# The first expert's slots are gathered by themselves, and parts of three weight matrices are loaded by transfers of their own

## The chip, the cores and the metric

The kernel runs on one core of one Trainium2 chip. The metric is the device time of one execution in microseconds (us). TensorE has two clock levels, 1.2 and 2.4 GHz; the profile shows the level that was granted as 0.50 or 1.00.

## What is computed

Two transformer layers over 256 tokens of width 1024, all in float32. The change lies in the second layer, and almost all of it in the mixture of 32 experts at its end:

```python
def hier_moe(h, w_group, b_group, w_expert, b_expert, w1, w3, w2):
    ...
    g_sel = jnp.argmax(g_logit, axis=-1)             # one of 4 groups
    ...
    top_p, top_i = lax.top_k(jax.nn.softmax(e_logit, axis=-1), EXPERT_TOPK)   # 2 of its 8 experts
    gate = g_w * top_p / jnp.sum(top_p, axis=-1, keepdims=True)
    ...
    def expert_block(args):
        xb, e = args
        hid = jax.nn.silu(xb @ w1[e]) * (xb @ w3[e])
        return hid @ w2[e]
    ...

def hybrid_layer(x, ...):
    ...
    x = x + mixed @ w_out
    x = x + hier_moe(rms_norm(x, g_ffn), w_group, b_group, w_expert, b_expert, w1, w3, w2)
    return x
```

Each expert has an up matrix pair w1 and w3 (1024 x 512) and a down matrix w2 (512 x 1024), each 2 MB (2.10 million bytes): 192 MB for 32 experts. The second matrix of the pair, w3, is the one that the title of the change calls the up matrix.

## The kernel before

**Dense part.** Both layers up to the experts go through `unit_plan`, a list of 1 MB weight units. SyncE (the `sp` program) loads unit u into a ring of three places (`arena` slots 1 to 3) once unit u-3 has been split (`load`, which waits on `lo_ready`), ScalarE and VectorE split it into a high and a low part, and TensorE (the `pe` program) multiplies. `step_plan` puts the other steps between the units. In the second layer the units `kiwi`, `qi` x2, `kb` x2, `qb` x2, `vb` x2 and so on come first; `rope_done` counts the rotated key and query blocks that VectorE has finished (line 2004), and the fourth is that of the first `kb` unit.

**Loads of the experts.** SyncE issues all of them, in the order of its program, and each waits for its buffer. Four sets of buffers serve the first four experts: `even_w` for expert 0, `odd_w` for 1, `third_w` for 2, `fourth_w` for 3. `odd_w[1]`, for w3 of expert 1, lies in `arena` slots 0 and 1; slot 1 is one of the ring's, slot 0 is not. The down matrix of expert 3 shares its buffer (`even_w[2]`) with that of expert 0, so its load waits for `e_y` 1, the end of expert 0's last matmul. The load of the first half of expert 4's w1 waits for `e_w1_half`, the middle of expert 0's w1; the second half for `e_w1`; its w3 for `e_up` 1, the end of expert 0's w3; its w2 for `e_y` 4. From expert 8 on a loop (`stream`) issues the three matrices of one expert after another, each as soon as the expert that used the buffer is through with it.

**Experts.** They go in eight groups of four (`QUAD`), with 32 slots for tokens each. `quad_body` on TensorE first gathers the tokens of the four experts together, in 16 calls of 128 x 128 weights (`n3g`) against the 128 columns of `one_hot` (line 1302; the profile counts two records for each float32 call); ScalarE and VectorE copy the result to `xg`. Then come, for each expert, w1 and w3 (line 1358), the gates of the four experts behind the first one's w3 (`spread_gates`, line 1326) or the sum of the expert before (`add_to_tokens`, line 1342), and w2 (line 1374). The first two quads are written out, the others run in a loop. Ahead of the first quad stands the choice of the experts: 36 columns of logits (`route_logits`, line 1167), a chain on VectorE, the ranks (lines 1284 to 1288) and `one_hot` (line 2309).

## Time and profile before

| what | us |
|---|---|
| median of 3 runs | 1076.07 (1074.75 to 1076.33) |
| the profiled execution, its time | 1076.97 |
| the profiled execution, its span | 1074.9 |
| TensorE busy in the span | 932.0 (87%) |
| weights loaded into TensorE | 767.0 (71%) |
| VectorE busy | 505.0 (47%) |
| ScalarE busy | 364.1 (34%) |
| bytes moved | 310.00 MB, mean 288 GB/s |
| start of the first gather | 631.43 |
| start of the last expert's w2 | 1062.50 |

The shares are means over stages of different kinds: up to about 580 us TensorE is busy without a break and the DMA engines about half of the time; later it is the other way round. Times in the rows are from the span's start.

### The profile page before, as it was taken

Reading aid. Unit: us, or ns where it says so; the run is one execution under the profiler, and the core shown is the slowest. Engines: PE = TensorE matmul, PEld = TensorE weight load, DVE = VectorE, ACT = ScalarE, POOL = GpSimd, SP = SyncE. Lnnn points to the kernel's source line nnn. Section 1 sums busy time; section 2 is a strip of 40 time slices with the busy share of each in tenths; the row PEclk is TensorE's granted clock in tenths of the full one; section 3 lists DMA queues with packets and bytes.
Section 4 is the critical chain, followed back from the end, with each engine's and each line's share of the span. In section 5 each row is a group of like instructions: output and inputs, shape, how many; then the busy total and the mean of one; then the engine's idle time right before and its main releaser. Section 6 shows DMA issues by size and latency. Waiting matters only on the chain.

```text
span 1074.9 us, 22614 instructions
## 1 busy us (share of the span) xinstructions
PE 932.0 (87%) x9976; PEld 767.0 (71%) x9976; DVE 505.0 (47%) x812; ACT 364.1 (34%) x517; POOL 32.6 (3%) x34
## 2 busy tenths in 40 slices
PE   9999999999999999999999988886766657676754
PEld 8998877888888888989777876665545546464642
DVE  5647768687676667889877651110000100010101
ACT  6445766454444345444666330000000000000001
POOL 1200002110000001000000000000000000000000
PEclk9999999999999999999999999998888988797988
DMA  9954434545555654444457999999999999999995
GB/s 330 309 176 165 152 130 163 172 162 196 195 183 169 211 160 157 158 157 157 158 180 285 392 399 425 422 427 426 427 426 429 428 429 429 429 429 429 428 429 209
DMA packets 86830, 310.00 MB, mean 288 GB/s; under 512 B 5612, under 2 KB 46264, under 8 KB 73976
## 3 DMA queue, kind: packets, MB, share of 16 engines
q1 hardware_dynamic: 84816, 304.20, 73.4%
q0 software_dynamic: 1056, 4.20, 1.2%
q8 instruction: 42, 0.69, 0.3%
q10 hardware_dynamic: 904, 0.81, 0.2%
q14 instruction: 12, 0.10, 0.0%
HBM read 308.15 MB, written 1.05 MB: 288 GB/s over the span
## 4 chain that ended last, share of the span: by engine, by line
PE 58%; issue 38%; DVE 2%; ACT 1%; POOL 1%; ACTq 0%; POOLq 0%; DVEq 0%
PE ps L879 13%; PE ps L881 12%; PE ps L880 12%; PE ps L1003 7%; PE ps L1005 4%; PE ps L1358 1%; PE ps L1152 1%; PE ps L1374 1%; PE ps L1140 1%; PE ps L1058 1%; ACT x_both L1582 1%; PE ps L1302 0%; PE ps L1064 0%; POOL stat L816 0%; PE ps L978 0%
## 5 line engine op out<-in xcount | busy, mean ns | idle before, releaser
L1358 PE MATMUL ps<-arena,xg 128*32 128x128 f32 x2816 | 108.9, 318 | 75.1 <-DMA arena<-in_w 72.7
L1742 DVE TENSOR_TENSOR w_split<-arena,w_split 128x2048 fp32r<-128x2048 f32 x70 | 159.3, 2287 | 28.3 <-ACT w_split L1419 27.8
L2328 DVE TENSOR_TENSOR hid<-silu_e,ps 128x128 f32<-128x128 f32 x32 | 12.1, 378 | 313.6 <-ACT silu_e L1691 313.6
L1358 PEld LDWEIGHTS ps<-arena,xg 128*32 128x32 f32 x2816 | 93.4, 128 | 92.5 <-DMA arena<-in_w 86.0
L1419 ACT ACTIVATE w_split<-arena 128x2048 fp32r<-128x2048 f32 x70 | 132.7, 1900 | 66.1 <-PE ps L881 57.9
L1003 PE MATMUL ps<-x_both,w_split 128*128 128x512 f32 x352 | 124.8, 398 | 0.0
L879 PE MATMUL ps<-w_split,x_both 128*128 128x512 f32 x256 | 102.2, 399 | 0.3 <-DVE w_split L1798 0.3
L880 PE MATMUL ps<-w_split,x_both 128*128 128x512 f32 x256 | 99.8, 390 | 0.0
L881 PE MATMUL ps<-w_split,x_both 128*128 128x512 f32 x256 | 99.8, 390 | 0.0
L1005 PE MATMUL ps<-x_both,w_split 128*128 128x256 f32 x352 | 98.8, 281 | 0.0
L1374 PE MATMUL ps<-arena,hid_T 128*32 128x256 f32 x960 | 68.0, 428 | 28.1 <-DMA arena<-in_w 26.9
L1691 ACT ACTIVATE silu_e<-ps 128x128 f32<-128x128 f32 x32 | 8.9, 277 | 238.4 <-PE ps L1358 238.4
L1003 PEld LDWEIGHTS ps<-x_both,w_split 128*128 128x128 f32 x352 | 66.1, 188 | 16.4 <-issue 0.3
L1374 PEld LDWEIGHTS ps<-arena,hid_T 128*32 128x32 f32 x960 | 33.1, 120 | 57.6 <-issue 37.2
L879 PE MATMUL ps<-x_both,w_split 128*128 128x256 f32 (+1 forms) x256 | 72.9, 285 | 0.9 <-DVE w_split L1742 0.7
L881 PE MATMUL ps<-x_both,w_split 128*128 128x256 f32 (+1 forms) x256 | 72.3, 283 | 0.0
L880 PE MATMUL ps<-x_both,w_split 128*128 128x256 f32 (+1 forms) x256 | 72.3, 282 | 0.0
L879 PE MATMUL ps<-w_split,o_hi 128*128 128x512 f32 (+1 forms) x176 | 68.2, 388 | 0.5 <-DVE gates L1960 0.5
L1752 DVE TENSOR_TENSOR w_split<-arena,w_split 128x2048 fp32r<-128x2048 f32 x24 | 55.0, 2293 | 26.3 <-ACT w_split L1429 25.0
L881 PE MATMUL ps<-w_split,o_lo 128*128 128x512 f32 (+1 forms) x176 | 67.1, 381 | 0.0
L880 PE MATMUL ps<-w_split,o_hi 128*128 128x512 f32 (+1 forms) x176 | 66.9, 380 | 0.0
L1005 PEld LDWEIGHTS ps<-x_both,w_split 128*128 128x128 f32 x352 | 66.5, 189 | 0.4
(325 smaller groups left out, 1471.4 us busy)
## 6 DMA issues: line engine op xcount, KB each, us to landing
arena<-in_w SPq DMA_DIRECT2D x71, 2048.0 KB, 26.0
arena<-in_w_in SPq DMA_DIRECT2D x41, 1024.0 KB, 5.1
even_w<-in_w SPq DMA_DIRECT2D x13, 2048.0 KB, 26.4
arena<-in_w_ffn_in SPq DMA_DIRECT2D x22, 1024.0 KB, 5.1
third_w<-in_w SPq DMA_DIRECT2D x6, 2048.0 KB, 16.6
arena<-in_w_ffn_out SPq DMA_DIRECT2D x11, 1024.0 KB, 4.9
arena<-in_w_out SPq DMA_DIRECT2D x8, 1024.0 KB, 6.4
arena<-in_w SPq DMA_DIRECT2D x6, 1024.0 KB, 7.5
```

What stands on the lines that cost most here:

```text
L879: mm(dst, l_hi, r_hi, start=start, stop=False)
L880: mm(dst, l_hi, r_lo, start=False, stop=False)
L881: return mm(dst, l_lo, r_hi, start=False, stop=stop)
L1003: mm(ps[:, bank + n, :], hi[:, c, col], x_both[:, c, :, :].rearrange("p a b -> p (a b)"), start=c == 0, stop=False)
L1005: last = mm(ps[:, bank + n, 0:T], lo[:, c, col], x_hi[:, c, :], start=False, stop=c == kc - 1)
L1058: mm(ps[:, bank, 0:P], ones, ones, start=True, stop=True)
L1358: last = mm(ps[SLOTS * g:SLOTS * g + SLOTS, 6, P * n:P * n + P], xg[:, c, SLOTS * e:SLOTS * e + SLOTS], places[n][:, c, P * g:P * g + P], ...
L1374: last = mm(ps[SLOTS * g:SLOTS * g + SLOTS, 7, 0:UC], hid_T[:, SLOTS * b:SLOTS * b + SLOTS], places[2][:, b, UC * g:UC * g + UC], start=b ...
L1419: fn(w_hi[:, u % 3, 0:n], ring[:, u % 3, 0:n], ACT.Copy).then_inc(hi_ready, 1)
L1742: v.tensor_tensor(w_lo[:, u % 3, 0:n], ring[:, u % 3, 0:n], w_hi[:, u % 3, 0:n].bitcast(F32), ALU.subtract).then_inc(lo_ready, 1)
L1752: v.tensor_tensor(w_lo[:, s, :], ring[:, s, :], w_hi[:, s, :].bitcast(F32), ALU.subtract)\
L2328: v.tensor_tensor(hid[:, :].rearrange("p (b i) -> p i b", b=4), silu_e[:, :].rearrange("p (i b) -> p i b", b=4), ps[:, 6, P:2 * P].rearran ...
```

## The change

It has five parts.

1. **First gather in two.** In the first quad TensorE gathers the 32 slots of expert 0 alone (`collect(0, SLOTS)`), then does its w1, then gathers the 96 slots of experts 1 to 3 (`collect(SLOTS, P)`), then its w3. The copies to `xg` on ScalarE and VectorE are split in the same way. Later quads gather as before.
2. **First half of expert 1's w3.** Its 1 MB goes to `arena` slot 0 right behind the load of unit `kiwi` + 7 and after a wait for `rope_done` 4, early in the second layer; the second half is issued where the whole was.
3. **First quarter of expert 3's w2.** Its 0.5 MB goes to a buffer of its own, `spare_w2`, right behind the load of expert 2's w2; the other three quarters are issued where the whole was. The room comes from putting `gate_e` where `masked_e` lay.
4. **Down matrix in two transfers.** In the loop of loads, which now goes by quads (8 to 31), the w2 of each quad's last expert comes as three quarters and a last quarter; TensorE waits for the last (`last_block`) only ahead of its fourth block. These are 6 more transfers.
5. **Counts.** The waits on `xg_half`, `xg_done`, `xg_part` and `xg_ready` are one higher from the second quad on.

```diff
@@ -436,13 +436,14 @@
     logits = moe("logits", [P, TB, 36])
     exp_in = moe("exp_in", [P, TB, 36])
     exp_out = moe("exp_out", [P, TB, 36])
+    masked_at = mo
     masked_e = moe("masked_e", [P, TB, EXPERTS + 6])
     left_e = moe("left_e", [P, TB, EXPERTS + 6])
     top2 = moe("top2", [P, TB, 8])
     pick_g = moe("pick_g", [P, TB, GROUPS])
     r_s = moe("r_s", [P, 16, TB])
     chosen = moe("chosen", [P, TB, EXPERTS])
-    gate_e = moe("gate_e", [P, TB, EXPERTS])
+    gate_e = moe("gate_e", [P, TB, EXPERTS], where=masked_at)
     rank = moe("rank", [P, TB, EXPERTS])
     slot_no = moe("slot_no", [P, SLOTS])
     one_hot = moe("one_hot", [P, TB, P])
@@ -454,6 +455,8 @@
     silu_e = moe("silu_e", [P, P])
     hid = moe("hid", [P, P])
     hid_T = moe("hid_T", [P, P])
+
+    spare_w2 = moe("spare_w2", [P, D])
 
     ps = nc.alloc_psum_tensor("ps", [P, 8, 512], F32)
 
@@ -552,6 +555,8 @@
     hot_ready, xg_done, xg_ready, gt_done, gt_ready = (sem(n) for n in ("hot_ready", "xg_done", "xg_ready",
                                                                         "gt_done", "gt_ready"))
     e_w1, e_w1_half = sem("e_w1"), sem("e_w1_half")
+    last_block = sem("last_block_w2_in")
+    odd_first, spare_in = sem("odd_w3_first_half"), sem("spare_quarter_in")
     e_up, e_silu, e_hid, e_hidT, e_y, e_yA = (sem(n) for n in (
         "e_up", "e_silu", "e_hid", "e_hidT", "e_y", "e_y_act"))
     gt_rest, xg_half = sem("gt_rest"), sem("xg_half")
@@ -723,6 +728,11 @@
             landing = (first_half, landed_w[0])[half][which]
             sp.dma_start(even_w[which][:, part, :], sources[which][:, e, part, :]).then_inc(landing, 16)
 
+        def odd_half(half):
+
+            part = slice(4 * half, 4 * half + 4)
+            sp.dma_start(odd_w[1][:, part, :], sources[1][:, 1, part, :]).then_inc((odd_first, landed_w[1][1])[half], 16)
+
         for u in range(S2 + 3 * (NF - 2), U):
             if u == second_merge + 1:
                 sp.wait_ge(o_done, 20)
@@ -735,6 +745,9 @@
             elif u == out20:
                 half_load(1, 1)
             load(u)
+            if u == first["kiwi"] + 7:
+                sp.wait_ge(rope_done, 4)
+                odd_half(0)
             if u in (out20, out20 + 1):
                 if u == out20:
                     sp.wait_ge(o_done, 28)
@@ -744,7 +757,7 @@
         sp.wait_ge(sum_T, 8)
         expert_load(1, odd_w, 0, landed_w[1][0])
         sp.wait_ge(lo_ready, U - 2)
-        expert_load(1, odd_w, 1, landed_w[1][1])
+        odd_half(1)
         sp.wait_ge(unit_done, U - 2)
         expert_load(2, third_w, 0, in_third3[0])
         sp.wait_ge(lo_ready, U)
@@ -753,6 +766,7 @@
         expert_load(2, third_w, 1, in_third3[1])
         sp.wait_ge(unit_done, U)
         expert_load(2, third_w, 2, in_third3[2])
+        sp.dma_start(spare_w2[:, :], sources[2][:, 3, 0, :]).then_inc(spare_in, 16)
         sp.wait_ge(route_T, 4)
         sp.wait_ge(sq_ready, 4)
         sp.wait_ge(seeded, 4)
@@ -764,7 +778,7 @@
         sp.wait_ge(e_up, 1)
         expert_load(4, even_w, 1, landed_w[0][1])
         sp.wait_ge(e_y, 1)
-        expert_load(3, fourth_w, 2, in_fourth[2])
+        sp.dma_start(fourth_w[2][:, 1:4, :], sources[2][:, 3, 1:4, :]).then_inc(in_fourth[2], 16)
         for which in range(3):
             sp.wait_ge((e_w1, e_up, e_y)[which], 2)
             expert_load(5, odd_w, which, landed_w[1][which])
@@ -778,17 +792,22 @@
             sp.wait_ge((e_w1, e_up, e_y)[which], 6)
             expert_load(7, odd_w, which, landed_w[1][which])
 
-        def stream(pass_, lo_pair):
-
-            with sp.Fori(lo_pair, EXPERTS // 2) as i:
-                for odd in range(2):
-                    e = sp.snap(i * 2 + odd)
-                    used = sp.snap(i * 2 + (pass_ * EXPERTS + odd - 1))
+        def stream(pass_, lo_quad):
+
+            with sp.Fori(lo_quad, EXPERTS // QUAD) as i:
+                for j in range(QUAD):
+                    e = sp.snap(i * QUAD + j)
+                    used = sp.snap(i * QUAD + (pass_ * EXPERTS + j - 1))
                     for which in range(3):
                         sp.wait_ge((e_w1, e_up, e_y)[which], used)
-                        expert_load(e, (even_w, odd_w)[odd], which, landed_w[odd][which])
-
-        stream(0, 4)
+                        if (j, which) == (QUAD - 1, 2):
+                            src = sources[2][:, bass.ds(e, 1), :, :].rearrange("p e c n -> p (e c) n")
+                            sp.dma_start(odd_w[2][:, 0:3, :], src[:, 0:3, :]).then_inc(landed_w[1][2], 16)
+                            sp.dma_start(odd_w[2][:, 3:4, :], src[:, 3:4, :]).then_inc(last_block, 16)
+                        else:
+                            expert_load(e, (even_w, odd_w)[j % 2], which, landed_w[j % 2][which])
+
+        stream(0, 2)
         sp.wait_ge(passes_ready, 1)
         n_pass = sp.value_load(passes_i[0:1, 0:1], min_val=1, max_val=T // SLOTS)
         with sp.If(n_pass > 1):
@@ -1294,16 +1313,20 @@
 
             if not looped:
                 pe.wait_ge(n3_ready, 2)
-            for half in range(2):
-                for tb in range(TB):
-                    if half == 0:
-                        pe.wait_ge(hot_part, q * 2 + (tb + 1))
-                    for i in range(4):
-                        last = mm(ps[:, 4 + half, P * i:P * i + P], n3g[:, tb, 4 * half + i, :], one_hot[:, tb, :],
-                                  start=tb == 0 and i == 0, stop=tb == 1 and i == 3)
-                if half == 0:
-                    last.then_inc(xg_half, 1)
-            last.then_inc(xg_done, 1)
+            first_quad = not looped and q == 0
+
+            def collect(lo, hi):
+
+                for half in range(2):
+                    for tb in range(TB):
+                        if half == 0:
+                            pe.wait_ge(hot_part, q * 2 + (tb + 1))
+                        for i in range(4):
+                            last = mm(ps[:, 4 + half, P * i + lo:P * i + hi], n3g[:, tb, 4 * half + i, :],
+                                      one_hot[:, tb, lo:hi], start=tb == 0 and i == 0, stop=tb == 1 and i == 3)
+                    last.then_inc((xg_half, xg_done)[half], 1)
+
+            collect(0, SLOTS if first_quad else P)
 
             def place_of(e):
 
@@ -1350,10 +1373,12 @@
                 for n in range(2):
                     if not looped and e == 0 and (q == 0 or n == 0):
                         pe.wait_ge(first_half[n], 16 * (q + 1))
+                    if first_quad and (e, n) == (1, 1):
+                        pe.wait_ge(odd_first, 16)
                     pe.wait_ge(landing[n], arrived)
                     for c in range(KC):
                         if e == 0 and n == 0 and c % 4 == 0:
-                            pe.wait_ge((xg_part, xg_ready)[c // 4], q + 1)
+                            pe.wait_ge((xg_part, xg_ready)[c // 4], q + 1 if first_quad else q + 2)
                         for g in range(4):
                             last = mm(ps[SLOTS * g:SLOTS * g + SLOTS, 6, P * n:P * n + P],
                                       xg[:, c, SLOTS * e:SLOTS * e + SLOTS], places[n][:, c, P * g:P * g + P],
@@ -1361,6 +1386,11 @@
                         if not looped and q == 0 and e == 0 and n == 0 and c == KC // 2 - 1:
                             last.then_inc(e_w1_half, 1)
                     last.then_inc((e_w1, e_up)[n], 1)
+                    if first_quad and (e, n) == (0, 0):
+                        collect(SLOTS, P)
+                if e == 0 and first_quad:
+                    for half in range(2):
+                        pe.wait_ge((xg_part, xg_ready)[half], 2)
                 if e == 0:
                     spread_gates()
                 else:
@@ -1370,9 +1400,15 @@
                 pe.wait_ge(landing[2], arrived)
                 pe.wait_ge(e_hidT, done + 1)
                 for b in range(4):
+                    if looped and (e, b) == (QUAD - 1, 3):
+                        pe.wait_ge(last_block, pe.snap(q * 16 - 16))
+                    w2_block = places[2][:, b, :]
+                    if first_quad and (e, b) == (3, 0):
+                        pe.wait_ge(spare_in, 16)
+                        w2_block = spare_w2[:, :]
                     for g in range(4):
                         last = mm(ps[SLOTS * g:SLOTS * g + SLOTS, 7, 0:UC],
-                                  hid_T[:, SLOTS * b:SLOTS * b + SLOTS], places[2][:, b, UC * g:UC * g + UC],
+                                  hid_T[:, SLOTS * b:SLOTS * b + SLOTS], w2_block[:, UC * g:UC * g + UC],
                                   start=b == 0, stop=b == 3, tile_position=(0, SLOTS * g))
                 last.then_inc(e_y, 1)
             add_to_tokens(QUAD - 1)
@@ -1684,8 +1720,13 @@
 
         def quad_body(q):
             e0 = act.snap(q * QUAD) if not isinstance(q, int) else 0
-            act.wait_ge(xg_half, q + 1)
-            fn(xg[:, 0:4, :].rearrange("p a b -> p (a b)"), ps[:, 4, :], ACT.Copy).then_inc(xg_part, 1)
+            act.wait_ge(xg_half, q + 1 if isinstance(q, int) else q + 2)
+            if isinstance(q, int):
+                fn(xg[:, 0:4, 0:SLOTS], in_chunks(4)[:, :, 0:SLOTS], ACT.Copy).then_inc(xg_part, 1)
+                act.wait_ge(xg_half, 2)
+                fn(xg[:, 0:4, SLOTS:P], in_chunks(4)[:, :, SLOTS:P], ACT.Copy).then_inc(xg_part, 1)
+            else:
+                fn(xg[:, 0:4, :].rearrange("p a b -> p (a b)"), ps[:, 4, :], ACT.Copy).then_inc(xg_part, 1)
             for e in range(QUAD):
                 act.wait_ge(e_up, e0 + (e + 1))
                 fn(silu_e[:, :], ps[:, 6, 0:P], ACT.Silu).then_inc(e_silu, 1)
@@ -2310,15 +2351,17 @@
                 dve.wait_ge(hot_part, q * 2 + (tb + 1))
             if not looped:
                 dve.wait_ge(xg_done, 1)
-                v.tensor_copy(flat(xg[:, 4:8, :]), ps[:, 5, :]).then_inc(xg_ready, 1)
+                v.tensor_copy(xg[:, 4:8, 0:SLOTS], in_chunks(5)[:, :, 0:SLOTS]).then_inc(xg_ready, 1)
                 gate_weights()
+                dve.wait_ge(xg_done, 2)
+                v.tensor_copy(xg[:, 4:8, SLOTS:P], in_chunks(5)[:, :, SLOTS:P]).then_inc(xg_ready, 1)
             for tb in range(TB):
                 hot = one_hot[:, tb, :].rearrange("p (e s) -> p e s", e=QUAD)
                 gate = gate_e[:, tb, bass.ds(at_e, QUAD)].unsqueeze(2).to_broadcast([P, QUAD, SLOTS])
                 ins = v.tensor_tensor(gated_hot[:, tb, :].rearrange("p (e s) -> p e s", e=QUAD), hot, gate, ALU.mult)
             ins.then_inc(hot_ready, 1)
             if looped:
-                dve.wait_ge(xg_done, q + 1)
+                dve.wait_ge(xg_done, q + 2)
                 v.tensor_copy(flat(xg[:, 4:8, :]), ps[:, 5, :]).then_inc(xg_ready, 1)
             else:
                 count_passes()
```

## Rows read from the trace of the kernel before

**Rows 1.** The page's row of DMA rates, 40 equal slices of the span.

```profile
GB/s 330 309 176 165 152 130 163 172 162 196 195 183 169 211 160 157 158 157 157 158 180 285 392 399 425 422 427 426 427 426 429 428 429 429 429 429 429 428 429 209
```

**Rows 2.** Waits from 684 to 1070 us: total, times, longest.

```profile
PE ps L1358 <- DMA arena<-in_w: 72.7, 29, 3.0
```

**Rows 3.** Timeline at the end, TensorE: start, us, count, idle before.

```profile
1057.58 3.48 PE L1358 MATMUL ps<-arena,xg 128*32 128x128 f32 x64 [2.94 <-DMA arena<-in_w]
...
1062.50 1.93 PE L1374 MATMUL ps<-arena,hid_T 128*32 128x256 f32 x32 [0.28 <-DMA arena<-in_w]
1064.93 1.15 PE L1342 MATMUL ps<-y_part,gate_T 32*128 32x256 f32 x16 [0.50 <-ACT y_part L1696]
```

**Rows 4.** Timeline, TensorE, first quad and the second quad's gather.

```profile
631.43 5.30 PE L1302 MATMUL ps<-one_hot,n3g 128*128 128x128 f32 x32 [0.29 <-DVE one_hot L2309]
636.66 2.00 PE L1358 MATMUL ps<-arena,xg 128*32 128x128 f32 x64
638.48 1.93 PE L1358 MATMUL ps<-even_w,xg 128*32 128x128 f32 x64
...
671.93 3.83 PE L1302 MATMUL ps<-one_hot,n3g 128*128 128x128 f32 x32
```

**Rows 5.** Windows: PE, PEld, DVE, ACT, POOL busy (count), clock, DMA share, GB/s.

```profile
631.50:632.50 1.00, 1.00 (x5) 1.00 (x6) 0.10 (x1) 0.00 (x0) 0.00 (x0) 0.50 1.00 426
635.00:636.00 1.00, 1.00 (x11) 1.00 (x10) 0.00 (x0) 0.98 (x2) 0.00 (x0) 1.00 1.10 459
637.50:640.50 3.00, 3.00 (x115) 2.80 (x108) 2.62 (x15) 0.03 (x1) 0.00 (x0) 1.00 0.68 197
```

**Rows 6.** Timeline, weight loads around a logits step.

```profile
614.59 1.09 PEld L1167 LDWEIGHTS ps<-w_route,n3T 128*128 128x128 f32 x8
615.60 0.19 PEld L879 LDWEIGHTS ps<-w_split,sum_hi 128*128 128x128 f32 x1
```

**Rows 7.** Issues of line 724 from 568.7 us, and time to landing.

```profile
L724 SPq DMA_DIRECT2D even_w<-in_w x2: 340/422/505, 568.7 to 569.6; - x2
...
DMA to landing us min/median/max: 5.3/7.4/9.6
```

**Rows 8.** Issue of expert 3's w3 and time to landing.

```profile
L717 SPq DMA_DIRECT2D extra_w<-in_w x1: 328/328/328, 626.3 to 626.3; - x1
...
DMA to landing us min/median/max: 13.6/13.6/13.6
```

**Rows 9.** Issues of the halves of expert 4's w1.

```profile
L724 SPq DMA_DIRECT2D arena<-in_w x2: 328/328/328, 637.8 to 638.7; - x2
...
DMA to landing us min/median/max: 6.7/7.5/8.3
```

**Rows 10.** Issue of expert 4's w3.

```profile
L717 SPq DMA_DIRECT2D even_w<-in_w x1: 327/327/327, 640.5 to 640.5; - x1
...
DMA to landing us min/median/max: 11.4/11.4/11.4
```

**Rows 11.** Issues of expert 6's w1 (656.6, the 21.0) and of expert 4's w2.

```profile
L717 SPq DMA_DIRECT2D third_w<-in_w x1: 328/328/328, 656.6 to 656.6; - x1
L717 SPq DMA_DIRECT2D arena<-in_w x1: 328/328/328, 670.4 to 670.4; - x1
...
DMA to landing us min/median/max: 13.6/17.3/21.0
```

**Rows 12.** Issues of the next two units behind `kiwi` + 7.

```profile
L676 SPq DMA_DIRECT2D arena<-in_w_in x2: 367/367/367, 438.8 to 443.9; - x2
...
DMA to landing us min/median/max: 5.0/5.2/5.4
```

**Rows 13.** Timeline, VectorE and ScalarE, second layer.

```profile
447.15 0.69 DVE L2004 TENSOR_TENSOR kb<-head_expo,head_right 128x512 f32<-128x512 f32 x1
...
456.85 2.29 DVE L1742 TENSOR_TENSOR w_split<-arena,w_split 128x2048 fp32r<-128x2048 f32 x1
...
466.14 1.91 ACT L1419 ACTIVATE w_split<-arena 128x2048 fp32r<-128x2048 f32 x1 [3.82 <-PE ps L881]
```

## The prediction

> **What bounds the kernel now.** I read the DMA rates of the page first. From about 590 us to the end the rate stands at 392 to 429 GB/s [rows 1], and it changes little whatever the engines do: this is a stream that never runs dry. The waits say the same from TensorE's side: behind 684 us it waits for a landing before its matmuls with w1 or w3 29 times, 72.7 us in all [rows 2]. So the end is set by the last landing, and a 2 MB matrix costs 2.10 MB / 429 GB/s = 4.9 us, 1 MB 2.45 us. Time can come only from three things: fewer bytes in the stream, fewer gaps in it, a shorter tail behind it.
>
> Windows show one gap. Between 637.5 and 640.5 us only 197 GB/s are moved [rows 5], (429 - 197) x 3.0 = 0.70 MB or 1.6 us of the stream too little. The reason stands in two views. Everything that could be issued ahead lands by 626.3 + 13.6 = 639.9 [rows 8]; the next load, the first half of expert 4's w1, needs the middle of expert 0's w1 and is issued at 637.8 [rows 9]. TensorE reaches that middle 1.0 us into line 1358, behind 5.30 us of gather [rows 4].
>
> At the end w3 of the last expert runs 1057.58 to 1061.06, and w2 starts at 1062.50, 0.28 us of that for its landing; the rest to the end of the span, 1074.9, is 12.4 us from there [rows 3]. The sum is a difference to the profiled execution, 1074.9 of span and 1076.97 us in all, which is 0.90 above the median of 1076.07; I put the difference on the median.
>
> **First gather in two.** It removes three quarters of the columns from the gather that stands before expert 0's w1 and adds 16 calls, 32 records, behind it. What does a record with 32 columns cost? The trace has no such gather, but the logits have 36 columns against the same 128 x 128 float32 weights: 8 weight loads take 15.60 - 14.59 = 1.01 us, 0.126 us each [rows 6]. With 128 columns a record costs 3.83 / 32 = 0.120 us [rows 4]. The weight load sets both. So the first gather stays at about 5.3 us, between 0.2 less and 0.4 more, and the issue at 637.8 doesn't move; the copies in front of w1 shrink, but w1's first half doesn't wait for them. The second gather costs 32 x 0.120 = 3.8 us (2.9 if it went by columns, three quarters of 3.83). It lies between expert 0's w1 and w3 and pushes back everything behind it on TensorE: the end of w3, with it the issue of expert 4's w3, from 640.5 [rows 10] to 644.3; likewise the load of expert 3's w2, and expert 4's w2 from 670.4 [rows 11] to 674.2. VectorE's second copy and gate products fit beside it.
>
> **What that does to the stream.** Part 2 takes 1 MB out of the full stretch before the gap and part 3 puts 0.5 MB into it, so the stream runs dry 1.2 us sooner, while its restart at 637.8 stays: the gap grows by 1.2 us. That eats part 2's gain, except that the slowest DMA engine has no backlog left at the restart. On an idle queue 1 MB lands 5.3 us behind its issue [rows 7], here it took 6.7 [rows 9]. The first half of expert 4's w1 lands at 643.1 to 644.5, the second 2.5 later. Then comes w3, issued at 644.3. The queue is nearly empty again: 5.3 + 2.45 = 7.75 to 6.7 + 2.45 = 9.15 us, 652.0 to 653.4, against 640.5 + 11.4 = 651.9 before [rows 10]. So here +0.1 to +1.5 (-0.5 with the cheap second gather, where the landing before sets it: 646.5 + 4.9 = 651.4); I take +0.7, the middle, since neither row is nearer. Without the added gather this load would have had 2 MB of cover ahead of it.
>
> **Fewer bytes.** Behind that point expert 3's w2 is 1.5 MB, not 2: -1.2 us. Its own quarter lies in the full stretch and is there long before 666 us. The stream is then at -0.5 (-1.7 to +0.3).
>
> **The next gate.** Expert 4's w2, issued at 674.2 instead of 670.4, would land on an empty queue at 681.9 to 683.4; it landed at 684.0, behind a queue that reached to 677.6 [rows 11], and the shifted stream brings it at 683.5. So the backlog covers it: 0, at most +0.5. If that cover were gone, 3.8 us more on TensorE would cost as much.
>
> **Six more transfers in the loop.** Two halves of 1 MB land 647.0 - 644.5 = 2.5 us apart [rows 9], a whole one takes 4.9: up to 0.1 us for each more, 0 to +0.6 in all. I take +0.2.
>
> **Tail.** The last w2 waited 0.28 us for its landing [rows 3]. With three quarters of it there 1.2 us sooner, that wait goes: -0.2. The gain depends on the clock: w3 took 3.48 us there, against 1.93 for the same work at the full level [rows 3, 4]; had it run so, hid_T would have been ready 1.55 us sooner and the three blocks could start 1.2 us earlier. Hence 0 to -1.2; I take -0.3, nearer to the row, which had the slow w3.
>
> **Early half of w3.** SyncE waits for `rope_done` 4, which comes at 447.84 [rows 13]; behind it stand the loads that were issued at 438.8 and 443.9 [rows 12]. The half lands at about 453.2, the first held load at 455.7, the next at 458.2. Splitting the first takes 1.9 us on ScalarE and 2.3 on VectorE, so it is ready at 459.9, and TensorE is through with the unit before it at 466.1 [rows 13]. About 6 us of slack, no cost. Were this cover gone, the 9.1 us of hold would show in part. On ScalarE and VectorE the index scores stand behind that split and are late by some 3 us; the split of the row ends at 459.1, 7 us ahead of its use [rows 13], which covers that.
>
> **Sum.** -0.5 + 0 + 0.2 - 0.3 = -0.6 us: 1076.07 - 0.6 = 1075.5. Own bounds: -1.7 - 1.2 = -2.9 and +0.3 + 0.5 + 0.6 = +1.4, that is 1073.2 to 1077.5.
>
> **Rivals.** *The gather goes by columns.* For it: the pass is written for this, and of the loads at half clock I have no row with few columns. Against it: the 0.126 us [rows 6]. Then the first gather takes 5.30 / 4 = 1.3 us, w1 of expert 0 starts 4.0 sooner, and the issue at 633.8 meets a queue that is busy to 638.7: no gap. Expert 4's w1 is there at 641.2 and 643.7, its w3, issued at 640.5 - 4.0 + 2.9 = 639.4, at 648.6, 3.3 us sooner; with the 1.2 us for the bytes and the -0.1 of transfers and tail -4.6: 1071.5 us. The Trainium skill (TensorE: Matmul & The Clock Gate, Back-to-back issue gap) gives 1 to 64 columns about 60 cycles from matmul to matmul and 128 columns 134, but for single matmuls, without the budget of weight loads; by the first figure the sum would be this rival's. The trace does not agree where each matmul has a load of its own.
>
> *The clock stays low.* This is the slower case. TensorE waited with little work ahead of the gather, began it at 0.50, and had 1.00 again from 635 us [rows 5]. The new gather keeps the array less busy: 32 columns for each load instead of 128. If that doesn't raise the clock, a record takes twice 0.120, 0.24 us, 7.7 us for the 32 instead of 5.3, and the first half of w1 takes 2.0 instead of 1.0: the issue comes at 641.2, w3's at 644.3 + 2.4 + 2.0 = 648.7, landing at 656.5 to 657.9, about +5.3 against 651.9. With -1.2 for bytes and -0.1: +4.0, 1080.1 us. It decides as soon as the rise comes more than about 2 us later. Against it: the weight loads run without a break, as before. No row shows so few columns at the lower level.
>
> *The wait on SyncE shows in the dense part.* It needs the 6 us of slack to be wrong; then some 2 to 3 us, 1078.
>
> *Each further transfer costs its fixed time.* The Trainium skill (DMA: Bandwidth & Descriptors, Anatomy of one DMA) counts 2.0 us fixed for each; six exposed ones would be +12, 1087.5 us. Against it: the 2.5 us between two landings [rows 9], which leaves 0.1 for it.
>
> **How the numbers follow.** My case 0.68, the gather by columns 0.14, the low clock 0.11, SyncE 0.05, the fixed time 0.02. The predicted time is that of the likeliest. For 8 in 10 I take my case's range, 1073.2 to 1077.5, and reach down to the fast rival, rounded out to 1071.3 and 1077.8; the low clock and the small ones stay outside. A measurement of this kernel tells about 0.2%, 2.15 us, from no change. Faster by more: the first rival, 0.14, and 0.13 of my case's 0.68 (its lower end, with the tail's full gain). Slower by more: the low clock 0.11, the fixed time 0.02, 0.02 of SyncE's and 0.05 of mine. Within: 0.53.
>
> **What would show it.** Right: the first gather takes 5 us or more for its 32 records, the second 3.6 to 4.0; the issue of expert 4's w1 stays within 0.5 us of 637.8 while everything ahead of it has landed about 1.2 us sooner; its w3 is issued at about 644.3 and lands 7.7 to 9.2 us later, with a dip of the DMA rate ahead of it; expert 4's w2 lands near 683.5; the last w2 starts without waiting for its landing; TensorE has no new wait from 440 to 590 us. Wrong: a first gather of 2 us, a clock of 0.50 behind 635 us, a landing of expert 4's w3 before 651 us, or a wait of TensorE for a split near 466 us. What I can't read from this trace is where TensorE's waits for nothing that the profile shows fall once its program is 64 instructions longer; such a wait between the second gather and w3 would push the stream back by its length.

## The result and the profile after

| | before | after |
|---|---|---|
| median, us | 1076.20 (1074.75 to 1076.72) | 1087.56 (1082.44 to 1091.81) |
| ratio, 95% interval | | 1.0107 (1.0084 to 1.0131) |
| profiled execution, span | 1074.9 | 1084.6 |
| expert 4's w2, issue and landing | 670.4, 684.0 | 679.0, 686.9 |
| expert 7's w1, issue and landing | 687.8, 698.7 | 695.6, 704.5 |
| packets of instructions | 42 | 60 |

The change costs 11.4 us by the medians, 9.7 between the two spans. The forecast was 1075.5 with a range up to 1077.8: it was wrong, in the direction too. The lines moved: the gather is now line 1325, w1 and w3 line 1383, the sum of the expert before line 1365, w2 line 1410, a whole load line 722.

TensorE's timeline after, where [rows 4] stood:

```profile
631.15 5.58 PE L1325 MATMUL ps<-one_hot,n3g 128*128 128x32 f32 x32 [0.29 <-DVE one_hot L2350]
636.66 3.34 PE L1383 MATMUL ps<-arena,xg 128*32 128x128 f32 x64
639.92 3.81 PE L1325 MATMUL ps<-one_hot,n3g 128*128 128x96 f32 x32
643.67 1.95 PE L1383 MATMUL ps<-even_w,xg 128*32 128x128 f32 x64
...
654.54 0.85 PE L1383 MATMUL ps<-arena,xg 128*32 128x128 f32 x20 [1.87 <-issue]
...
662.63 3.33 PE L1383 MATMUL ps<-third_w,xg 128*32 128x128 f32 x69 [2.39 <-issue]
...
675.54 0.71 PE L1365 MATMUL ps<-y_part,gate_T 32*128 32x256 f32 x6 [1.65 <-issue]
```

The two gathers take what the forecast gave them: 5.58 us for the first, 3.75 for the second. w1 starts at 636.66 in both traces. But w1 takes 639.92 - 636.66 = 3.26 us, not 1.82: with the second gather's 3.75, w3 starts 5.2 us later than in [rows 4]. And the waits for nothing that the profile shows ("issue", idle time that no engine and no landing ends) are 5.91 us from 640 to 680, not 2.8. So expert 4's w2 is issued 8.6 us later.

Windows after, with the columns of [rows 5]:

```profile
631.50:632.50 1.00, 1.00 (x12) 1.00 (x11) 0.00 (x0) 0.00 (x0) 0.00 (x0) 1.00 1.02 381
632.50:635.50 3.00, 3.00 (x18) 3.00 (x17) 0.00 (x0) 0.28 (x1) 0.00 (x0) 0.54 1.05 436
635.50:639.50 4.00, 4.00 (x62) 3.72 (x66) 2.13 (x11) 0.00 (x0) 0.00 (x0) 0.50 0.37 160
639.50:645.00 5.50, 5.50 (x96) 5.21 (x92) 1.12 (x5) 1.77 (x2) 0.00 (x0) 1.00 0.96 317
```

The clock is at its lower level from 632.7 to 639.5 us, 6.8 us instead of the 3.4 of before (631.1 to 634.6), and nearly all of w1 lies in it. Unlike before, the gather starts at the full level (1.00 in the first row), and the clock falls within it.

Issues of expert 4's w3, of its w2 and of expert 7's w1 after, each with its time to landing:

```profile
L722 SPq DMA_DIRECT2D even_w<-in_w x1: 328/328/328, 645.7 to 645.7; - x1
...
DMA to landing us min/median/max: 8.9/8.9/8.9
...
L722 SPq DMA_DIRECT2D arena<-in_w x1: 328/328/328, 679.0 to 679.0; - x1
...
DMA to landing us min/median/max: 7.9/7.9/7.9
...
L722 SPq DMA_DIRECT2D arena<-in_w x1: 327/327/327, 695.6 to 695.6; - x1
...
DMA to landing us min/median/max: 8.9/8.9/8.9
```

And the load that the forecast never looked at, expert 7's w1, in the kernel before:

```profile
L717 SPq DMA_DIRECT2D arena<-in_w x1: 328/328/328, 687.8 to 687.8; - x1
...
DMA to landing us min/median/max: 10.9/10.9/10.9
```

Call a wait of SyncE ahead of a load a gate, and the loads that are still queued when the gate opens the backlog. Where the load ahead lands within 0.4 us of the issue, so that the queue is as good as empty, a 2 MB load lands 7.9 to 8.5 us behind its issue (7.9 at expert 4's w2 here, 8.1 and 8.5 at expert 7's w1 in gather_warm17 and gather_alone below). What a landing takes beyond that is the cover that the backlog gives a late issue: before, 13.6 - 7.9 = 5.7 us at expert 4's w2 [rows 11], but at most 10.9 - 7.9 = 3.0 us at expert 7's w1. After, the load ahead of expert 4's w2 lands at 679.1, with the issue at 679.0: nothing is left. At expert 7's w1 the load ahead lands at 698.0, 2.4 us behind the issue, and that isn't enough: it lands 6.5 us after the load ahead, where a full queue takes 4.9. The DMA rate (last column) falls at both places after, where before had 429 and 433 GB/s:

```profile
675.00:682.00 7.00, 5.97 (x62) 3.52 (x62) 0.19 (x1) 0.38 (x1) 0.00 (x0) 0.76 0.74 253
695.00:700.00 5.00, 3.25 (x100) 2.71 (x89) 0.38 (x1) 0.28 (x1) 0.00 (x0) 1.00 0.82 272
```

The account of the 9.7 us, by landings: the load ahead of expert 4's w2 +1.5 (677.6 to 679.1), expert 4's w2 +2.9, the load ahead of expert 7's w1 +4.2 (693.8 to 698.0), expert 7's w1 +5.8 (698.7 to 704.5). Expert 10's w3, ten matrices on, +4.9 (749.1 to 754.0), since before had one late step of 1.5 us there and after one of 0.7. From there to the end +4.8: the 64 landings behind it stand 4.9 us apart before, without exception; after, seven of them come 0.6 to 1.1 us late (764.7, 785.4, 815.4, 836.0, 964.1, 1004.1, 1014.6), 6.0 us in all, and the stretch from the last landing to the end is 1.2 us shorter (11.3 us instead of 12.5). What else is there in these turns of the loop? The DMA queue of instructions from 770 to 1040 us, after:

```profile
q8 instruction: 18, 0.29, 0.5%
```

Columns: packets, MB, share. Before, this queue moves nothing there: its last packet is between 760 and 770 us. After, it starts again twice, at 780 and 958 us, and both times TensorE's next gather waits long:

```profile
784.78 6.18 PE L1325 MATMUL ps<-one_hot,n3g 128*128 128x128 f32 x32 [7.00 <-issue]
...
962.61 6.03 PE L1325 MATMUL ps<-one_hot,n3g 128*128 128x128 f32 x32 [6.56 <-issue]
```

Two turns of the loop are fetched anew, with packets from 780 to 830 and from 958 to 1009 us. Six of the seven late landings, 5.1 of the 6.0 us, lie there or up to 6 us behind; the one at 764.7 does not. A packet is 0.29 MB / 18 = 16 KB. The Trainium skill (Runtime: NRT & Kernel Launch, Instruction fetch mechanics) says that an engine's instructions are refilled in blocks of 16 KiB by the sequencer's own DMA queue, and that a taken branch out of what is held forces such a fetch. The size of the packets agrees. The Trainium skill calls the cost of going on to the next block, in that section, mostly hidden, and the fetch behind a branch a stall. TensorE's waits of 7.00 and 6.56 us at the two turns fit such a stall; the queued loads hide them, but not the landings that come late.

The tail after, beside [rows 3]:

```profile
1068.52 1.96 PE L1383 MATMUL ps<-arena,xg 128*32 128x128 f32 x64 [1.69 <-DMA arena<-in_w]
1070.41 1.15 PE L1365 MATMUL ps<-y_part,gate_T 32*128 32x256 f32 x16
1072.26 1.93 PE L1410 MATMUL ps<-arena,hid_T 128*32 128x256 f32 x32 [0.71 <-DMA arena<-in_w]
```

w3 ran at the full clock this time, and w2 waits 0.71 us for the landing of its three quarters at 1072.1, where the forecast said it wouldn't wait. The last quarter lands at 1073.4, so w2 starts 1.1 us ahead of the last landing; before, it started behind it. From the start of w2 to the end it is 12.3 us, as before (12.4), and from the last landing 11.3 instead of 12.5.

### The profile page after: what moved, and what is told of

It reads as the page before. It is cut to its first block, busy times and chain, and to the rows that moved or that the text cites. A ratio compares the mean times of both kernels' runs of the same rounds, so it can differ in the third digit from the quotient of the medians.

```text
span 1084.6 us, 22711 instructions
## 1 busy us (share of the span) xinstructions
PE 936.8 (86%) x10008; PEld 773.0 (71%) x10008; DVE 504.9 (47%) x813; ACT 364.9 (34%) x518; POOL 32.6 (3%) x34
## 4 chain that ended last, share of the span: by engine, by line
PE 57%; issue 38%; ACT 1%; DMA 1%; DVE 1%; POOL 0%; SPq 0%; POOLq 0%; ACTq 0%; DVEq 0%
PE ps L898 12%; PE ps L900 12%; PE ps L899 12%; PE ps L1022 7%; PE ps L1024 4%; PE ps L1383 2%; DMA arena<-in_w_in 1%; PE ps L1325 1%; PE ps L1171 1%; PE ps L1159 1%; PE ps L1410 1%; ACT x_both L1618 1%; PE ps L1077 0%; PE ps L1186 0%; PE ps L997 0%
## 5 line engine op out<-in xcount | busy, mean ns | idle before, releaser
L1383 PE MATMUL ps<-arena,xg 128*32 128x128 f32 x2816 | 105.7, 310 | 66.1 <-DMA arena<-in_w 54.5
```

The source lines that it names most:

```text
L1383: last = mm(ps[SLOTS * g:SLOTS * g + SLOTS, 6, P * n:P * n + P], xg[:, c, SLOTS * e:SLOTS * e + SLOTS], places[n][:, c, P * g:P * g + P], ...
```

## The experiments

**Which part of the change is it?** The change with the gather whole; the gather's split alone; the parts of w2 in the loop alone; the two early loads alone.

```diff
# whole_gather: the change, but
-            collect(0, SLOTS if first_quad else P)
+            collect(0, P)
-                    if first_quad and (e, n) == (0, 0):
-                        collect(SLOTS, P)
# whole_gather: the copies to xg whole too, the waits to match
# gather_alone: before with the two collect calls, the four copies and their waits
# w2_parts_alone: before with the two-part load in stream() and its wait
# early_loads_alone: before with odd_half(0), odd_half(1) and spare_w2
```

The last three also keep the loop of loads by quads and the place of `gate_e` from the change.

Expected, the change with the whole gather: 

> The changed kernel with the first gather left whole (16 calls, 128 columns, ahead of expert 0's w1); early half, early quarter and the down matrix in two transfers stay. Theory 1 (the split gather makes the loss: its second part and the low clock push back TensorE in the first quad, and the stream of loads runs dry): the loss goes, and 1.2 us for the bytes and some tenths of tail remain, 1074 to 1075.5 us. Theory 2 (the loop makes it: six more transfers and a longer loop body on TensorE, whose instructions are fetched again): still 1080 us or more, with waits of TensorE for nothing that the profile shows of up to 7 us in the loop.

The split alone: 

> The kernel before with the split gather alone. Theory 1: about 1084 to 1088 us, the landing of expert 4's w3 at 654 or later, that of expert 4's w2 at 687 or later. Theory 2: within 3 us of 1076, since the loop is as before.

The parts of w2 alone: 

> The kernel before with the down matrix of each looped quad's last expert in two transfers, nothing else. Theory 1: 1075.5 to 1076.5 us. Theory 2: 1080 us or more, with the waits in the loop and with more bytes on the instruction queue than 0.69 MB.

The early loads alone: 

> The kernel before with the early half of expert 1's w3 and the early quarter of expert 3's w2 alone. Both theories: 1.2 us fewer behind the gate at expert 0's w1, the gap ahead of it 1.2 us longer, 1074.3 to 1075.3 us; instruction queue 0.69 MB. If SyncE's wait in the dense part costs something, 1077 or more, with waits of TensorE for a split near 466 us.

Measured, as ratios to before: whole gather 0.9998 (0.9989 to 1.0007), split alone 1.0104 (1.0083 to 1.0126), parts of w2 alone 1.0001 (0.9992 to 1.0009), early loads alone 1.0011 (1.0002 to 1.0019). The split makes the whole loss, as the first theory had it. The six more transfers cost nothing. The early loads don't gain their 1.2 us in the median. Their trace does show it in the stream: expert 7's w1 lands at 696.7 instead of 698.7, and the last landing comes at 1060.4 instead of 1062.4. But in this execution the last w2 ran at the lower clock (3.55 us instead of 1.93), and the span is 1075.1 us all the same. Why the median has no gain stays open.

The split alone, TensorE's timeline:

```profile
631.96 6.33 PE L1316 MATMUL ps<-one_hot,n3g 128*128 128x32 f32 x32 [0.29 <-DVE one_hot L2334]
638.22 3.64 PE L1372 MATMUL ps<-arena,xg 128*32 128x128 f32 x64
641.79 4.34 PE L1316 MATMUL ps<-one_hot,n3g 128*128 128x96 f32 x32
646.07 1.96 PE L1372 MATMUL ps<-even_w,xg 128*32 128x128 f32 x64
```

Here the clock is low from 632.7 to 642.9 us, 10.2 us long. From the start of the gather to the issue of expert 4's w2 it is 48.8 us, 9.9 more than before: 1.0 the first gather, 1.8 w1, 4.3 the second gather, 3.1 more waits for nothing shown, less 0.3 elsewhere.

**Is it the clock, or the order?** The first part with all 128 columns again; and the second part moved behind expert 0's w3, so that expert 4's w3 isn't held back by it.

```diff
# gather_twice
-            collect(0, SLOTS if first_quad else P)
+            collect(0, P)
# rest_behind_w3 (and VectorE's second copy behind the gate products)
-                    if first_quad and (e, n) == (0, 0):
+                    if first_quad and (e, n) == (0, 1):
                         collect(SLOTS, P)
```

Expected: 

> The kernel before with the split gather, but the first part gathers all 128 columns again, as before; the second part (96 columns) stays and only repeats work. So TensorE has the same records as in the split gather, without few-column records ahead of w1. Theory A (the low clock that the 32-column records leave makes much of the loss): 4 to 6 us better than the split gather, 1080 to 1082 us, clock back to 1.00 inside the first gather. Theory B (the 32 added records and where they stand make the loss, the clock adds little): 1084 us or more.

> The split gather alone, with its second part behind expert 0's w3 instead of ahead of it. Theory C (the load of expert 4's w3, held back by the second part, is what dries the stream): most of that part of the loss goes, 1080 us or less. Theory D (what counts is TensorE's total up to the end of expert 3's w2, which frees the buffer of expert 4's w2 and so the chain behind it): as the split gather, 1084 to 1086 us.

Measured: 1.0075 (1.0047 to 1.0103) and 1.0076 (1.0054 to 1.0098). With 128 columns in the first part the clock is back at 635.0, and gather and w1 take 5.44 and 1.96 us. The ratio is 0.3% below that of the split alone, but the two intervals overlap (1.0083 to 1.0126 there), so what the clock's part costs in the median isn't shown; most of the loss stays without it. The median, 1082.50 us, lies between the two expectations. With the second part behind w3, expert 4's w3 is issued at 643.5 instead of 648.1, but its w2 at 679.5 and expert 7's w1 at 697.9, about as late as with the split alone (680.8 and 699.0): the later gates decide, not this one. The time, 1084.16 us, is that of the theory by which TensorE's total counts.

**Warming before the choice, and 64 instructions more.** On the kernel before, 17 instead of 10 calls of warming work; 64 empty instructions; 16 small matmul calls of 64 instructions in TensorE's idle time ahead of the ranks. And the 17 calls with the split gather.

```diff
# warm17, gather_warm17
-CHOICE_WARM = 10
+CHOICE_WARM = 17
# nops64
+        for _ in range(64):
+            pe.nop()
# pad64
+        for _ in range(16):
+            mm(ps[0:32, 5, 0:8], ones[:, 0:32], ones[:, 0:8], start=True, stop=True)
```

Expected: 

> The kernel before with 17 instead of 10 warming calls ahead of the choice of the experts, so that TensorE has no idle stretch there. If the clock at the first gather matters, the gather takes 3.8 us in every execution and the time falls by 0.5 to 1.5 us, to about 1075; if the stream's total alone counts, nothing changes.

> The kernel before with 64 instructions without work on TensorE ahead of the wait for the choice of the experts, as many as the split gather adds (32 records, each a weight load and a matmul). Theory E (the added waits for nothing that the profile shows come from where the blocks of instructions end): these waits between 640 and 680 us grow from 2.8 to about 6 us in all and the time rises by 1 to 3 us. Theory F (they come from the stream and the delay alone): 1075.5 to 1076.5 us and waits of about 3 us.

> The kernel before with 16 small matmul calls (32 columns of weights, 8 of data; 64 instructions as the split gather adds) in the idle time of 1.65 us ahead of the ranks. If TensorE's waits for nothing that the profile shows grow because the program is longer and its parts lie at other places: such waits of 5 to 6 us between 640 and 680 us in place of 2.8, and a ratio of 1.002 to 1.004. If those waits belong to the split gather itself: 2.8 to 3.5 us and a ratio of 1.000. A third way: the pad changes the clock ahead of the gather; then the gather takes 3.8 or 5.3 us and that is seen by itself.

> The kernel before plus the split gather alone, with 17 calls of warming work in front of the choice in place of 10, so that the clock is full when the gather starts (with the whole gather and 17 calls it ran at the full clock, 3.81 us). If the low clock is a large part of the loss: first gather about 3.8 us in place of 6.3, expert 0's w1 about 1.95 us, first gather to the issue of expert 4's w2 some 45 us in place of 48.8, ratio about 1.006. If the few columns pull the clock down by themselves, it falls to 0.50 again within the first gather and w1, and the ratio stays at 1.010. If the loss is only the second gather's time on the path, it stays 3.8 us late and the ratio is 1.004 plus what the warming itself costs (0.0013).

Measured: 17 calls 1.0013 (1.0005 to 1.0022), empty instructions 0.9997 (0.9988 to 1.0006), small matmuls 1.0020 (1.0007 to 1.0033), 17 calls with the split 1.0140 (1.0125 to 1.0155). The trace with the empty instructions has as many instructions on TensorE as before (22614): they aren't in it, and the run says only how well a ratio repeats. The small matmuls do shift the program. TensorE's timeline with them:

```profile
649.79 0.85 PE L1360 MATMUL ps<-arena,xg 128*32 128x128 f32 x19 [1.61 <-issue]
...
657.88 2.16 PE L1360 MATMUL ps<-third_w,xg 128*32 128x128 f32 x68 [2.35 <-issue]
...
664.25 3.47 PE L1360 MATMUL ps<-extra_w,xg 128*32 128x128 f32 x117 [0.65 <-issue]
...
671.00 0.70 PE L1344 MATMUL ps<-y_part,gate_T 32*128 32x256 f32 x5 [2.22 <-issue]
```

That is 6.8 us of such waits up to 680, where before has 2.8; expert 7's w1 is issued 4.1 us later, and the time is 0.2% up. That fits the expectation for a longer program. The queue of instructions points the same way: in the changed kernel the three waits begin at 652.7, 660.2 and 673.9 us, and a packet of instructions starts at 652.1, 660.3 and 673.1. But these waits alone don't set the time. In the profiles with a whole gather they range from 2.8 us (before) over 5.2 (parts of w2 alone, 1.0001) to 7.3 (17 calls, 1.0013), and the run with the empty instructions, the same program as before, has 3.8. So the split gather's 3.1 us more lie within what other small changes bring, and which part of them its 64 instructions cause isn't shown.

With 17 calls and the whole gather the clock is full from 629.9 us on and the gather takes 3.81 us. With 17 calls and the split:

```profile
630.77 4.58 PE L1316 MATMUL ps<-one_hot,n3g 128*128 128x32 f32 x32 [0.29 <-DVE one_hot L2334]
635.28 3.64 PE L1372 MATMUL ps<-arena,xg 128*32 128x128 f32 x64
638.85 4.48 PE L1316 MATMUL ps<-one_hot,n3g 128*128 128x96 f32 x32
```

The gather starts at the full clock, which falls at 633.4, in the middle of the 32-column records, and is back at 640.3. So the quiet time ahead of the gather isn't needed for the fall. The other profiles bear this out. In nine of the 18 TensorE has 1.6 us of idle time ahead of the ranks, in the other nine at most 0.11 us. Of the latter nine, the three with 32 columns (after, its second profile, gather_warm17) see the clock fall 1.4 to 2.7 us into the gather and stay low for 6.8 us; the five with 64 or 128 columns (warm17, nops64, the parts of w2 alone, the early loads alone, split64) see no fall there. In the ninth, pad64, small matmuls with 8 columns fill that time, and the clock falls 0.3 us into a gather with 128 columns, for 3.4 us. Each of these is one execution.

The ratio of 1.0140 is above all three expectations. From the landing of expert 10's w3 to the end this kernel takes 334.9 us, the split alone 327.4: five turns of its loop are fetched anew (see the table below).

**64 and 64 columns.**

```diff
# split64 (the copies likewise)
-            collect(0, SLOTS if first_quad else P)
+            collect(0, 2 * SLOTS if first_quad else P)
```

Expected: 

> The kernel before plus the split gather, but with 64 columns in the first part and 64 in the second. A record is bound by its weight load at both sizes, so at one clock this takes as long as 32 and 96. If the few columns delay the rise of the clock: the first gather takes 5.3 to 5.8 us in place of 6.3, w1 some 2 us in place of 3.6, and the ratio lies between 1.0075 (128 columns in the first part) and 1.010 (32). If the columns make no difference to the clock, everything is as with 32: 6.3 us, 1.010.

Measured: 1.0090 (1.0070 to 1.0109). In its profile the low stretch came ahead of the gather (625.5 to 628.9), and both gathers take 3.76 and 3.79 us at the full clock. So a record costs the same 0.12 us with 64 columns. For the clock it is one of the five above: after had its low stretch at the same place (625.9 to 629.3) and fell again in the gather with 32 columns, this one with 64 didn't. The profiled execution is one of the shorter, with a span of 1080.2 us; the median time is 1084.64.

**What a us costs at this place.** The second part with 4 of its 32 records (experts 1 to 3 get only a part of their tokens' values), and the second part computed twice.

```diff
# rest_short
-                        collect(SLOTS, P)
+                        for half in range(2):
+                            mm(ps[:, 4 + half, SLOTS:P], n3g[:, 0, 4 * half, :], one_hot[:, 0, SLOTS:P],
+                               start=True, stop=True).then_inc((xg_half, xg_done)[half], 1)
# rest_more: the same 16 calls once more, ahead of collect(SLOTS, P)
```

Expected: 

> The kernel before plus the split gather alone, but the second part shrinks to 4 of its 32 records, so that experts 1 to 3 get wrong tokens. It takes 28 records of 0.120 us, 3.4 us, from the path between the first gather and expert 4's w2 and leaves the first gather as it is. If the second gather's time counts one for one at the end: 3.4 to 3.8 us below the split gather alone, ratio about 1.007. If that time is covered by the queued loads, as forecast: no difference, 1.010. If the clock and the waits for nothing that the profile shows are all of the loss, also 1.010.

> The kernel before plus the split gather alone, with the second part computed twice: 32 more records, 3.8 us more between the first gather and expert 4's w2, the output unchanged. One for one: 3.8 us above the split gather alone, ratio about 1.014. Covered: 1.010. The slope from the short second part over the split gather alone to this one tells what a us of TensorE's work costs there.

Measured: 1.0031 (1.0019 to 1.0044) and 1.0159 (1.0146 to 1.0173), against 1.0104 for the split alone. The second gather isn't covered: 28 records less, 3.4 us of work, bring 7.9 us; 32 more cost 5.9. Neither is one for one or what was expected (1.007 and 1.014), and two other things move with it in the traces. Without most of the second gather the waits for nothing shown are 3.8 us, not 5.9; with twice of it they are 2.7 to 4.2. And the program with twice of it fetches instructions in the loop over and over, as its waits from 700 to 1040 us show (total, times, longest):

```profile
PE ps L1316 <- issue: 50.7, 10, 5.7
```

The kernel with the short second part is also the nearest to the delay that the forecast had in mind: expert 4's w2 is issued at 674.1 (though the clock is low for 10.2 us in it), and it costs 3.3 us (1.0031) all the same. Expert 4's w2 lands at 685.6 there, 1.6 us late, and expert 7's w1 at 701.7, 3.0 late.

**Second profiles.** The fetching in the loop differs between kernels with the same loop (the split alone, with 17 calls, with the second part twice). Does it belong to the program or to the execution?

Expected: 

> The changed kernel once more, for a second profile. In the first one the instruction queue moved 60 packets in place of 42, and five loads in the expert loop landed 0.7 to 1.2 us later than the step of 4.9 us. If the number belongs to the program: 60 again, and a span near 1084.6 us. If it belongs to the execution: another number, and a span that is lower by some 5 us with 42 packets and higher with 88.

> The split gather alone once more, for a second profile. In the first one the instruction queue moved 42 packets, as before. If the number belongs to the program: 42 and a span near 1084.4 us. If to the execution: possibly 60 or 88 and a span of 1086 to 1091 us. The clock's low stretch at the first gather may also have another length; then the gather's own time shows it.

> The split gather with its second part twice, once more. In the first profile 88 packets of instructions, and landings in the loop that come 1.5 us late at every second turn. If the number belongs to the program: 88 again and a span near 1091.9 us. If to the execution: another number, with 42 a span near 1083 us.

Measured: spans 1081.4, 1082.1 and 1093.3 us with 51, 43 and 88 packets; the first profiles had 1084.6, 1084.4 and 1091.9 with 60, 42 and 88. Both: twice the second gather gives 88 each time, the changed kernel one turn fetched anew where it had two. Over all profiles with the split gather, and two without:

| kernel | expert 7's w1 issued | expert 10's w3 landed | packets | span | span less that landing |
|---|---|---|---|---|---|
| before | 687.8 | 749.1 | 42 | 1074.9 | 325.8 |
| pad64 | 691.9 | 750.4 | 42 | 1077.6 | 327.2 |
| rest_short | 690.6 | 750.6 | 42 | 1078.1 | 327.5 |
| gather_alone | 699.0 | 757.0 | 42 | 1084.4 | 327.4 |
| gather_alone_again | 694.1 | 754.5 | 43 | 1082.1 | 327.6 |
| gather_twice | 694.4 | 753.0 | 43 | 1079.7 | 326.7 |
| rest_behind_w3 | 697.9 | 756.1 | 51 | 1085.5 | 329.4 |
| after_again | 694.6 | 752.9 | 51 | 1081.4 | 328.5 |
| after | 695.6 | 754.0 | 60 | 1084.6 | 330.6 |
| split64 | 690.1 | 749.7 | 60 | 1080.2 | 330.5 |
| gather_warm17 | 695.4 | 753.6 | 88 | 1088.5 | 334.9 |
| rest_more | 695.6 | 755.5 | 88 | 1091.9 | 336.4 |
| rest_more_again | 698.2 | 758.5 | 88 | 1093.3 | 334.8 |

From the same landing on, every kernel moves the same weights. The last column follows the packets: 326 to 328 us with 42 or 43, 329 with 51, 331 with 60, 335 to 336 with 88. This is a reading of 13 profiles; no experiment changed the fetching by itself, and what makes a turn of the loop be fetched anew stays open. The last column also holds the stretch behind the last landing, 11.3 to 14.3 us in these profiles. The seven kernels with a whole gather all had 42; the five that the table leaves out take 326.1 to 327.9 us.

## Why the prediction was wrong

**The step that failed** is "So the backlog covers it: 0, at most +0.5". The queue was read rightly in [rows 11], but expert 4's w2 was issued at 679.0 and not at 674.2, as the queue ran out (679.1), and landed at 686.9, 3.4 us behind the forecast's 683.5. The step also stopped one gate too early. The next wait of SyncE, for expert 5's w1 before expert 7's w1 is loaded, hangs on the same TensorE path, which meanwhile holds the second quad's gather, and had at most 3.0 us of cover. The issue comes 7.8 us late there, and the landing +5.8. The prediction did say that without the cover 3.8 us of TensorE would cost as much; it took the cover of one gate for that of all.

**The size of the delay** was the second error, and the larger one by an estimate: 3.8 us expected at expert 4's w2, 8.6 measured. With 3.8 us, expert 4's w2 would have landed at 674.2 + 7.9 = 682.1 or up to 0.6 later, ahead of the 684.0 of before, and expert 7's w1, issued at 691.6, at 700.5 with the 8.9 us that it took after: +1.8, and a sum of 1077.3, still inside the range. The 3.3 us of the kernel with the short second part say that it may be more. Of the 4.8 us that the delay is larger, 1.4 us is w1 at the lower clock, 3.1 the longer waits for nothing shown; the second gather's own 3.75 us was right. The clock was a rival with a chance of 0.11. Its mechanism came in part: the clock fell, though 1.6 us into the gather. Its argument against, that the weight loads run without a break as before, is what the runs refute: in all nine profiles with 32 columns in the first gather the clock was low for 6.8 or 10.2 us at it, in the four with 128 columns and a low stretch at its start (before, whole_gather, gather_twice, pad64) for 3.4. The waits were named at the end of the prediction as what it couldn't read, but had no term and no room in the range.

**Fetching in the loop**, with 5.1 us of late landings in the profiled execution, was not thought of.

**What held.** The records don't go by columns, so that rival fell: from start to start they stand 0.11 us apart at the full level and 0.21 at the lower one, with 32 columns (after: 14 steps in 1.56 us, 16 in 3.41) as with 128. Wholly at the lower level the 32 records with 32 columns take 7.00 us (rest_behind_w3), against the rival's 7.7. The fewer bytes count behind the gap: expert 3's w2 lands 1.7 us late where the w3 ahead of it was 2.7 late. Expert 4's w3 lands 8.9 us behind its issue, on a queue that is nearly empty, within the 7.75 to 9.15 that were worked out. The issue of expert 4's w1 moved from 637.8 to 638.7, 0.9 and not 0.5, since its half of w1 ran at the lower clock. SyncE's wait for the rotated keys cost nothing that shows, and the six transfers nothing, so a fixed time for each is not exposed in a full queue. The 2.0 us of the Trainium skill (DMA: Bandwidth & Descriptors, Anatomy of one DMA) are given there for transfers on the gpsimd path, while SyncE issues these. The gain in the tail came in the trace, at the far end of its bound: 11.3 us behind the last landing, where the split alone, whose last w2 also waits for its landing (0.64 us), has 12.7. It isn't in the median of the parts of w2 alone (1.0001).

**Left open:** the split alone and the change with all parts differ by 0.03% only, though the early loads alone cost 0.1%, and the spans of one kernel differ by 1.4 to 3.2 us between two profiles; how much of the loss in the median is fetching in the loop can't be said, since a median is not a profile. No version was found that beats the kernel before.

## What to carry to other kernels

Where a stream of loads is fed by gates that open with an engine's progress, list every gate up to the point where the backlog is long again, each with its cover (time to landing less that of a load on an empty queue), before a us on that engine is costed at nothing; the smallest cover decides, not the next one, and the cover is to be held against the whole delay, with what the clock and the waits for instructions may add. Splitting a matmul by columns saved nothing here, where each call has its own weights to load: it cost the second set of loads in full, and the part with few columns brought the clock down for what followed. Added instructions cost a little of their own in code that is run through once, next to a full DMA queue: 0.2% for 64 of them, 0.1% for seven warming calls.

## What the runs showed of the hardware

- Float32 records against 128 x 128 weights stand 0.11 us apart at the full clock and 0.21 at the lower level, with 32 as with 128 columns (at the full clock with 64 and 96 too). With 32 columns TensorE is busy all the time and the clock falls even from the full level (at 633.4 us, 2.7 us into such a gather), in three profiles of three; with 64 or 128 columns in none of five. The Trainium skill (TensorE: Matmul & The Clock Gate, Part 1: The HAM clock gate) calls the upper level the busy state, which activity brings about; a TensorE that the profile shows as fully busy (3.00 of 3.00 us) was nevertheless at 0.54.
- Instructions come by DMA in packets of 16 KB. Straight code next to a full DMA queue has waits for nothing that the profile shows, 2.8 to 7.3 us in 40 with a whole gather, and the three of the changed kernel begin within 0.8 us of such a packet's start.
- A loop that was fetched once may be fetched again, in one to five of its later turns, and it differs between kernels with the same loop: 42 and 43 packets with the split alone, 88 with 17 calls on top. In each such turn TensorE waits some 6 to 10 us at the gather, which the queued loads cover, and landings in these turns come late, 2.3 and 2.8 us in the two turns of the changed kernel's first profile, and are never made up. Whether the fetching makes them late isn't shown.
